# Sample score and value products in one step each of an attention head, in a hybrid decoder layer

## The reference

```python
z = jnp.einsum('bqhd,bkhd->bhqk', q, k) * (SB_HEAD_DIM ** -0.5)
z = z + sb_bias[None, :, None, None]
mask = k_pos[None, :] < q_pos[:, None]
log_keep = jnp.where(mask, jax.nn.log_sigmoid(-z), 0.0)
after = lax.cumsum(log_keep, axis=3, reverse=True) - log_keep
w = jnp.where(mask, jnp.exp(jax.nn.log_sigmoid(z) + after), 0.0)
return jnp.einsum('bhqk,bkhd->bqhd', w, v)
```

## Time and profile before

| | us |
|---|---|
| median of 3 runs | 5007.54 |
| lowest and highest run | 4987.62, 5008.25 |
| the profiled execution | 5001.89 |
| its span | 5000.0 |
| TensorE busy in the span | 4677.6 |
| VectorE busy | 2859.6 |
| ScalarE busy | 1316.0 |
| GpSimd busy | 782.6 |

### The profile page before, as it was taken

How to read it: one execution, slowest core, us unless ns; L and a number is a source line. 1 busy time by engine, 2 the same in 40 slices (tenths; PEclk the granted TensorE clock), 3 DMA queues, 4 the chain that set the end, 5 groups by cost and what they waited for, 6 DMA issues and landing times. The chain is left out here.

```text
span 5000.0 us, 70223 instructions
## 1 busy us (share of the span) xinstructions
PE 4677.6 (94%) x26702; PEld 2940.9 (59%) x26702; DVE 2859.6 (57%) x5220; ACT 1316.0 (26%) x1829; POOL 782.6 (16%) x743
## 2 busy tenths in 40 slices
PE   5999989999778799899999999999997999999996
PEld 4666644555676465566666666666664555555553
DVE  3456414433355434314666766667543989889884
ACT  2223213332110000211444444444222222222221
POOL 0000100000000001000000000000002766666640
PEclk6999987876676899899999999999998999999998
DMA  4443532211233344223455555545445888888861
GB/s 152 163 160 122 175 103 64 69 56 54 83 107 105 136 170 176 75 68 130 169 194 191 180 190 184 205 176 189 168 155 211 311 301 294 292 297 300 293 231 72
DMA packets 367537, 846.13 MB, mean 169 GB/s; under 512 B 35986, under 2 KB 198418, under 8 KB 358482
## 3 DMA queue, kind: packets, MB, share of 16 engines
q1 hardware_dynamic: 251122, 472.45, 27.7%
q0 software_dynamic: 72352, 272.81, 15.7%
q10 hardware_dynamic: 43840, 97.93, 5.2%
HBM read 665.05 MB, written 178.03 MB: 169 GB/s over the span
## 5 line engine op out<-in xcount | busy, mean ns | idle before, releaser
L364 PE MATMUL dot_ps<-h_parts,u_parts 128*128 128x384 f16 (+1 forms) x9216 | 1452.9, 317 | 7.2 <-PEq L1846 4.5
L364 PEld LDWEIGHTS dot_ps<-h_parts,u_parts 128*128 128x128 f16 x9216 | 892.5, 98 | 498.3 <-issue 6.5
L364 PE MATMUL totals_ps<-act_parts,v_parts 128*128 128x416 f16 x6144 | 1083.8, 340 | 33.3 <-DVE act_parts L2728 33.2
L364 PEld LDWEIGHTS totals_ps<-act_parts,v_parts 128*128 128x128 f16 x6144 | 601.5, 98 | 514.3 <-issue 36.4
L377 PE MATMUL in_ps<-h_parts_in,in_parts 128*128 128x384 f16 (+1 forms) x3168 | 492.3, 318 | 5.3 <-DVE in_parts L693 4.5
L2443 DVE SCALAR_TENSOR_TENSOR u_parts<-u_chunks,units,u_parts 128x1024 f16<-128x1024 f32 x126 | 161.8, 1284 | 516.4 <-ACT u_parts L2227 516.4
L2236 ACT ACTIVATE gelu<-dot_ps,units 128x384 f32<-128x384 f32 (+1 forms) x384 | 215.9, 563 | 808.0 <-PE dot_ps L364 807.9
L377 PEld LDWEIGHTS in_ps<-h_parts_in,in_parts 128*128 128x128 f16 x3168 | 309.2, 98 | 182.5 <-DVE in_parts L693 4.6
L2795 POOL DMA_INDIRECT row_value<-tmp_g_rows,row_g x256 | 307.6, 1202 | 394.1 <-POOLq L2101 316.2
L2684 ACT ACTIVATE v_parts<-v_group,units 128x1024 f16<-128x1024 f32 x128 | 136.6, 1137 | 768.0 <-PE totals_ps L364 712.9
L2739 DVE SCALAR_TENSOR_TENSOR h<-totals_ps,sum_unit,h 128x416 f32<-128x416 f32 x388 | 247.6, 647 | 140.7 <-PE totals_ps L364 137.2
(11 more groups left out here) (340 smaller groups left out, 5598.8 us busy)
## 6 DMA issues: line engine op xcount, KB each, us to landing
u_chunks<-in_u SPq DMA_DIRECT2D x128, 512.0 KB, 5.6
v_sweep<-in_v SPq DMA_DIRECT2D x128, 512.0 KB, 4.7
v_group<-in_v SPq DMA_DIRECT2D x32, 2048.0 KB
tmp_g<-gelu ACTq DMA_DIRECT2D x128, 416.0 KB, 2.7
tmp_w<-h POOLq DMA_DIRECT2D x26, 2048.0 KB, 8.4
w_groups<-tmp_w SPq DMA_DIRECT2D x32, 1664.0 KB
gelu_in<-tmp_g SPq DMA_DIRECT2D x32, 1664.0 KB
merge_sweep<-in_u POOLq DMA_DIRECT2D x64, 512.0 KB, 5.5
```

The lines of the kernel that those rows point to most:

```text
L364: mm = pe.matmul(bank, left(x), right(y), start=first and x == 0 and y == 0, stop=last and x == 1)
```

## The change

The four calls of `past_scores` at steps 2 to 5, each over two pages, become one call over all eight pages at step 3. The four calls of `past_values` at steps 6 to 9, each for one column block, become four calls in a row at step 7.

```diff
@@ -1010,10 +1010,11 @@
                         new_scores()
                     if seq is None and n == 4:
                         new_sums()
-                    if 2 <= n <= 5:
-                        past_scores(i, u, (2 * n - 4, 2 * n - 3))
-                    if 6 <= n <= 9 and seq is not None:
-                        past_values(seq, i - 1 + u, 1 - u, n - 6)
+                    if n == 3:
+                        past_scores(i, u, range(NPAGE))
+                    if n == 7 and seq is not None:
+                        for c in range(NC_):
+                            past_values(seq, i - 1 + u, 1 - u, c)
                     if n == 11:
                         past_sums(i, u)
```

## The result

The changed kernel takes 5053.8 us (median of 4 runs, 5052.3 to 5063.4), where the kernel before took 4998.3 beside it: a ratio of 1.0111, 95% interval 1.0087 to 1.0135. It is 55 us slower. The forecast was 5001, 7 us faster than before, and the range ended at 5045. The profiled execution took 5052.3 us with a span of 5050.5.

What follows compares the result with a forecast made beforehand. TensorE was taken as the bound, 54.3 us per head at full level plus lower-clock time. Terms: -9 us over seven heads, +6 for further stretches, -4 for the first head, so -7 us: 5001 us, range 4965 to 5045.

Steps and rivals of the forecast that it cites:

- What bounds the stage: Attention heads: TensorE is the bound, 54.3 us per head at full level, the rest time spent at the lower clock.
- Waits moved: TensorE's queue waits ahead of the score and value groups move with them: 0 us taken, bound 4.9.
- gaps opened: Steps 4 to 6, 8 and 9 lose their filler: 0 us taken, 2.2 us at the other end.
- VectorE's wait for the scores: At VectorE's step 6, 20.6 us in 8 places: goes away, and nobody gains.
- The bursts' own time: Steps 3 and 7: 3.6 and 4.5 us at full level, then 7.4 and 7.3 us at the lower.
- The return after the score burst: Dense work behind step 3's burst: level back after 5.5 us, lower end 1.5.
- The 6.8 us at the start stay: nothing there is changed: Start of each head: the lower-level stretch keeps its 6.8 us.
- After the value burst: Dense work behind step 7's burst: level back after 4.5 us, lower end 1.5.
- further stretch in every second head: Steps 4 and 5, too short to bring the level back: 3.4 us more at the lower level, 6 us in all.
- First head: Its 4.9 us wait for the pages goes: 4 us gained, bounds 4.9 gained to 3.5 lost.
- Rival 1: Steps 3 and 7: both bursts run wholly at the lower level, +37 us, 5045 us; chance 0.13.
- Rival 4: Steps 3 and 7: bursts without a gap hold the clock up, 4907 us; chance 0.03.

Runs made afterwards that it cites:

- The joined kernels: Five kernels, the one before or with moved bursts, issuing the next head's first two score products in steps 10 and 11: 4999.9 to 5037.8 us.
- Halved groups: Against the kernel before, each narrow group cut in two, half before and half behind the step's value product, at steps 2 to 9: 5060.1 us, ratio 1.0101.
- the values-only kernel: Against the kernel before, only the value groups gathered at step 7, scores left at steps 2 to 5: 5062.3 us, ratio 1.0130.

## Why the prediction was wrong

**What bounds the stage: right.** A head was 52.9 us of full-level TensorE time, near the 54.3 of before, and the rest was the clock. *Waits moved*, *gaps opened*: right, waits at 12.9 us and none in steps 4 to 6 or 8 and 9. VectorE's wait for the scores is gone and gained nothing, as said.

**The bursts' own time: right.** The score bursts of heads 2 to 8 took 10.0 to 11.5 us, mean 10.8, forecast 3.6 + 7.4; the value bursts 12.2 to 13.5, mean 12.9, forecast 4.5 + 7.3.

**The return after the score burst: the step that failed.** "So I take 5.5 us after the score burst." It was 14.5 to 14.7 us in three heads and 18.4 to 19.1 in four, 16.9 on average: 11.4 more at the lower level, half of it time, is about 40 us over seven heads. The value came from the 3.4 us behind one group and the 6.8 us stretch at the head's start, where products are as short. In six of the seven heads before the start did take 6.8, but that didn't carry over to another place. The 17.0 us stretch over steps 4 and 5 stood in the same table, and I charged it to the two narrow groups within it. With the groups gone, steps 4 to 6 by themselves took until step 7 or into it to bring the level back. Moving the burst in front of step 7 cut the return to 4.5 to 6.9 us in six of seven heads, and the time was that of before.

**"The 6.8 us at the start stay: nothing there is changed": the second.** The stretch at the start was 13.7 us in four heads, 10.2 in two and absent in one, 10.7 on average, where before it was 6.8 in six heads and 13.7 in one. The instructions there are the same and their time at the lower level was not; why, no run shows. It was 10.2 or 13.7 us in the kernel almost without narrow products too. Against the 7.8 of before this is 2.9 us more at the lower level per head, about 10 us of time over seven. The joined kernels put about 19 us on it, the most uncertain number here.

**After the value burst**: forecast 4.5, measured 5.1 to 6.6, mean 5.7. In lower-level time the fourth head was 13.6 + 8.8 + 18.5 + 11.2 + 5.9 = 58.0 us and the mean head 10.7 + 7.5 + 16.9 + 9.9 + 5.7 = 50.7, where the forecast had 31.5, and 33.2 with its further stretch in every second head.

**First head**: forecast 4 us gained, measured 5 lost (67.0 to 72.0). The wait for the pages went from 4.9 to 2.9 only, since the dense steps ahead of it now ran at the full level, and the burst ran wholly at the lower one:

```profile
733.25 13.76 PE L978 MATMUL zp_ps<-qz,h 128*128 128x16 f32 x64 [2.86 <-DMA h<-in_cache_k]
```

Rival 1 gave 5045 us, near the result, but for a reason that the trace denies: after the first head the bursts didn't run wholly at the lower level. Rival 4 is denied as well: 8.8 and 11.2 us of burst without a gap ran at 0.50. So this trace disagrees with the rule on idle gaps in the Trainium skill, "TensorE: Matmul & The Clock Gate", section "HAM oscillation", taken as the whole rule.

## What to carry to other kernels

When TensorE's clock falls inside a busy stage, price thin work by what follows it, not only by its own length: the cost is the stretch until wide, uninterrupted products have brought the level back. Put such work directly in front of the widest products: here that took the return from 13 us and more to under 7 in 13 of 14 heads. It only repaired the loss; no placing tried here was faster than the one of before. Don't carry the length of a return from one place of the program to another, and read it in every head and not in one.

## What the runs showed that I had not expected

A head's own work doesn't fix its level. Halved groups left one head at 64.7 us and another, with the same work, at 85.5. And a change in steps 7 to 9 lengthened stretches in steps 0 to 6 of the next head: the values-only kernel's 17.0 and 23.8 us stand where nothing was edited. The price of one edit is then likely not a property of that edit alone: 27 and 61 us for the two parts, 55 for both.
